# Strassen steps in w_down: where they stand in a group, and how many there are

## The reference, cut to what matters

```python
def conv_ffn(h, w_up, conv_w, conv_b, w_down):
    u = h @ w_up
    ...                                    # depthwise convolution of width 3 over tokens
    gate, val = jnp.split(y, 2, axis=-1)   # 5632 columns each
    return (jax.nn.silu(gate) * val) @ w_down
```

## Time and profile before

| | us |
|---|---|
| median of three runs | 2383.92 |
| lowest and highest | 2383.77, 2384.22 |
| profiled execution, whole | 2383.82 |
| its span in the trace | 2382.0 |

### The profile page before, as it was taken

The page is one execution under the profiler, slowest core; times in us unless marked ns, Lnnn a source line. Parts: engine busy times, 40 slices in busy tenths (PEclk is TensorE's granted clock), DMA queues, the critical chain, the costliest instruction groups (busy, mean ns, idle before and its releaser), DMA issues.

```text
span 2382.0 us, 30675 instructions
## 1 busy us (share of the span) xinstructions
PE 2376.1 (100%) x12581; PEld 2034.5 (85%) x12581; DVE 1700.7 (71%) x1804; ACT 1217.8 (51%) x1427; POOL 0.2 (0%) x4
## 2 busy tenths in 40 slices
PE   9999999999999999999999999999999999999999
PEld 8888888888888888888888888888888888888887
DVE  6565666666568868868768667855778778886788
ACT  5444454554545445445445555555555455545554
POOL 0000000000000000000000000000000000000000
PEclk9999999999999999999999999999999999999999
DMA  7566556565565665655665555555555655565555
GB/s 253 160 187 196 166 186 196 191 188 196 187 186 178 219 215 186 216 182 197 200 192 189 184 185 160 170 184 186 186 182 192 201 189 174 186 219 187 187 173 181
DMA packets 238039, 452.14 MB, mean 190 GB/s; under 512 B 16569, under 2 KB 20779, under 8 KB 237771
## 3 DMA queue, kind: packets, MB, share of 16 engines
q1 hardware_dynamic: 237147, 449.07, 58.1%
q10 hardware_dynamic: 752, 1.12, 0.1%
HBM read 446.46 MB, written 3.67 MB: 189 GB/s over the span
## 4 chain that ended last, share of the span: by engine, by line
PE 97%; DVE 2%; ACT 1%; DMA 0%; issue 0%; SPq 0%; DVEq 0%; ACTq 0%
PE PS L72 97%; DVE WL L72 1%; ACT WH L72 0%; DVE PT L72 0%; DMA RAW<-in_w_in 0%; DVE TB L72 0%; DVE PB L72 0%; DVE TA L72 0%; ACT TB L72 0%; DVE TC L72 0%; DVE SEL L72 0%; DVE MHL L72 0%; ACT TA L72 0%; DVE XT L72 0%; SPq L72 0%
## 5 line engine op out<-in xcount | busy, mean ns | idle before, releaser
L72 DVE TENSOR_TENSOR WL<-RAW,WH 128x1024 fp32r<-128x1024 f32 (+1 forms) x844 | 1002.0, 1204 | 513.5 <-ACT WH L72 511.1
L72 PE MATMUL PS<-XHL,WH 128*128 128x512 f32 x3984 | 1252.7, 396 | 0.3 <-DVE XHL L72 0.3
L72 ACT ACTIVATE WH<-RAW 128x1024 fp32r<-128x1024 f32 (+1 forms) x845 | 868.9, 1043 | 736.6 <-PE PS L72 723.4
L72 PEld LDWEIGHTS PS<-XHL,WL 128*128 128x128 f32 x3968 | 745.4, 188 | 176.0
L72 PE MATMUL PS<-XHL,WL 128*128 128x256 f32 x3968 | 779.7, 278 | 0.0
L72 PE MATMUL PS<-WH,MHL 128*128 128x512 f32 x2000 | 624.0, 390 | 0.0
L72 PEld LDWEIGHTS PS<-XHL,WH 128*128 128x128 f32 x3984 | 606.6, 188 | 4.4 <-issue 0.8
L72 PEld LDWEIGHTS PS<-WH,MHL 128*128 128x128 f32 x2000 | 375.4, 188 | 77.7
L72 PE MATMUL PS<-WL,MHL 128*128 128x512 f32 x1000 | 389.1, 389 | 0.0
L72 PEld LDWEIGHTS PS<-WL,MHL 128*128 128x128 f32 x1000 | 187.8, 188 | 38.3
L72 ACT ACTIVATE MHL<-TA 128x1024 fp32r<-128x1024 f32 x33 | 35.1, 1063 | 121.7 <-DVE TA L72 121.7
(11 more groups left out here) (150 smaller groups left out, 1211.6 us busy)
## 6 DMA issues: line engine op xcount, KB each, us to landing
RAW<-in_w_ff SPq DMA_DIRECT2D x256, 512.0 KB, 4.2
RAW<-in_w_in SPq DMA_DIRECT2D x224, 512.0 KB, 3.8
RAW<-in_w_up SPq DMA_DIRECT2D x176, 512.0 KB, 4.3
RAW<-in_w_down SPq DMA_DIRECT2D x88, 512.0 KB, 4.5
RAW<-in_w_mix_out SPq DMA_DIRECT2D x32, 512.0 KB, 3.9
RAW<-in_w_out SPq DMA_DIRECT2D x32, 512.0 KB, 3.6
RAW<-in_w_conv_out SPq DMA_DIRECT2D x16, 512.0 KB, 3.5
RAW<-in_w_attn_out SPq DMA_DIRECT2D x16, 512.0 KB, 4.3
```

Of the source, the lines that this page charges most:

```text
L72: ins = step[1](*step[2], **step[3])
```

## The change

The table `SEVEN` gets one tuple of pairs for each of the two groups of a part, instead of one for both. In ff both are as before. In the second and third part the steps move from the fifth and sixth pair to the fourth and sixth in the first group, and to the second, fourth and sixth in the other. In the short part the first group keeps its step at the fourth pair, and the second group gets one at the second pair beside it. The sums of activations are made for the union of both groups' pairs (`union`), each in a slot of its own: AXH and AXL have three slots instead of two, and AS moves into SQ to make room.

```diff
-SEVEN = {"ff": (2, 4), "down8": (4, 5), "down6": (3,)}
+SEVEN = {"ff": ((2, 4), (2, 4)), "down8": ((3, 5), (1, 3, 5)), "down6": ((3,), (1, 3))}
...
-            AXH = sb("AXH", [P, 2, 4, P], f32r, c=c)
-            AXL = sb("AXL", [P, 2, 4, P], f32r, c=c)
-            AS = sb("AS", [P, 4, P], c=c)
+            AXH = sb("AXH", [P, 3, 4, P], f32r, c=c)
+            AXL = sb("AXL", [P, 3, 4, P], f32r, c=c)
             EV = sb("EV", [P, 2, 512], c=c)
-            sb("QK2pad", [P, 4096 - 1536 - 2048], c=c)
...
+        AS = SQ[:].rearrange("p (a b) -> p a b", a=4)
...
+        def union(name):
+            return sorted({n for g in SEVEN[name] for n in g})
+
-        def pairs(w, row0, kcs, col0, name):
+        def pairs(w, row0, kcs, col0, name, g):
...
-                    seven = n in SEVEN[name]
+                    seven = union(name).index(n) if n in SEVEN[name][g] else None
                     steps.append((seven, len(ents), kcs[2 * n:2 * n + 2]))
-                    if seven:
+                    if seven is not None:
                         ents.extend((what, first) for what in ("left", "b22", "t13", "t24"))
...
-            sevens = [n for n, st in enumerate(steps) if st[0]]
+            sevens = [n for n, st in enumerate(steps) if st[0] is not None]
...
-                    i = sevens.index(n)
+                    i = seven
                     o, c = n == sevens[0], n == sevens[-1]
...
-            for i, pair in enumerate(SEVEN[name]):
+            for i, pair in enumerate(union(name)):
                 if pair // 2 == half_seg:
                     sums_x(i, 2 * (pair % 2), tok, after)
                     yield
```

More of the change, by code:

```diff
@@ L238, in weight_order @@
                 for g in range(2 if seg < 3 else 1):
-                    pairs(io["w_ff2"][0], 2048 * seg, k16, 1024 * g, "ff")
+                    pairs(io["w_ff2"][0], 2048 * seg, k16, 1024 * g, "ff", g)
             for g in (2, 3):
@@ L258, in weight_order @@
                     pairs(io["w_down_2"][0], 512 * g0, list(range(4 * (g1 - g0))), 1024 * g,
-                          f"down{2 * (g1 - g0)}")
+                          f"down{2 * (g1 - g0)}", g)
             return len(units)
@@ L511, in group_item @@
             mid = dict(mid)
-            sevens = [n for n, st in enumerate(steps) if st[0]]
+            sevens = [n for n, st in enumerate(steps) if st[0] is not None]
             ends = [None, None]
             for n, (seven, e, kcs) in enumerate(steps):
-                if not seven:
+                if seven is None:
                     for half in range(2):
@@ L603, in sums_x @@
             v = V.step(tt, AS[:, 3, :], a12, AS[:, 1, :], sub)
-            a = A.step(act, AXH[:, seven], AS[:], AF.Copy, after=[v, ax_free.get(seven)])
-            tok[seven] = V.step(tt, AXL[:, seven], AS[:], AXH[:, seven].bitcast(f32), sub, after=[a])
+            a = A.step(act, AXH[:, seven], AS, AF.Copy, after=[v, ax_free.get(seven)])
+            tok[seven] = V.step(tt, AXL[:, seven], AS, AXH[:, seven].bitcast(f32), sub, after=[a])
         def group(w, row0, kcs, g, name):
-            steps = pairs(w, row0, kcs, 1024 * g, name)
+            steps = pairs(w, row0, kcs, 1024 * g, name, g)
             group_col[id(steps[0])] = 1024 * g
```

## The result

| | before | after |
|---|---|---|
| median of the unprofiled runs, us | 2384.04 | 2393.64 |
| lowest and highest, us | 2383.77, 2385.09 | 2390.47, 2394.07 |
| profiled execution: whole, span, us | 2383.82, 2382.0 | 2393.97, 2392.2 |

The change costs 9.6 us. The ratio is 1.0037, 95% interval 1.0026 to 1.0048. I had forecast 2388.9, half of that, and a range up to 2391.2. The sign and the place are as forecast; a second cost comes on top of the wait.

A forecast was written before the change was run, and what follows sets the result against it. The prediction took PE to bound the kernel. Matmuls saved (-2.04), stalls won (-1.1) and waits for PSUM (+8.2) gave +5.06 us on 2383.82, so 2388.9 us, range 2385.5 to 2391.2.

The forecast's parts named there:

- the nine matmuls: PE, whole kernel: three more Strassen steps, each three matmuls or 0.68 us less, take off 2.04 us.
- The two stalls: w_down, first groups of second and third parts: PE's waits for WL shrink, winning 0.54 and 0.56 us, together 1.1.
- The wait for PSUM: Second groups' second pair: PE waits for DVE to empty four banks, 2.67, 2.19 and 3.37 us, together 8.2.
- E: Start of DVE's emptying of the first group's last step; 1834.62 us forecast in the short part, later events counted from it.
- The clock: Behind the second groups' waits: no cost in the sum; every us at the lower level would cost half a us.
- rival 4: Second pair: wait grows by a late load, 0.5 to 1.2 us a part, or clock falls; 2390.4 to 2392.4, chance 0.12.
- Rivals 2 and 3: Second pair: no wait, 2380.5 us, chance 0.08 (2); half of the wait, 2385.0 us, chance 0.13 (3).
- The chances of sign: Whole kernel: slower by over 0.2% (above 2388.7 us) 0.52, within 0.2% 0.46, faster 0.02.

The follow-up runs named there:

- third_pair: Changed kernel with the second groups' first step at the third pair instead of the second, as many steps: 2381.81 us, ratio 0.9990 to the kernel before.
- moves_only: Changed kernel without added steps: fourth and sixth pair in both groups of the long parts, short part as before: 2382.88 us, ratio 0.9994 to before.
- after_again: The changed kernel itself, run and traced once more: 2394.07, 2393.76, 2390.62, 2390.57 and 2394.12 us.
- The filler kernels: Changed kernel with 8 or 4 matmuls of zeros in the wait before the second group's first step: 2389.47 us with 8, 2389.11 with 4.
- evac_first: Changed kernel with the first group's banks emptied before the split of t13 enters DVE's queue: 2384.00 us, ratio 1.0000 to the kernel before.
- spread4: third_pair with the long parts' second group at third, fifth and sixth pair, and a fourth slot for activation sums: 2382.90 us, ratio 0.9995 to before.
- short_only: Changed kernel with the long parts' steps as before; only the short part has its additional step: 2386.1 us, ratio 1.0011 to the kernel before.

## Why the prediction was wrong

**The bound, and the nine matmuls.** Right. PE is the bound, and steps without a wait are worth what was summed: the short part of third_pair lasts 1873.50 - 1810.23 = 63.27 us, 0.67 less than in before, where 0.68 was forecast.

**The two stalls.** Right: 1.1 us forecast, 1.2 measured in moves_only. The third part's stall went whole, where 0.2 us of it was expected to stay.

**The wait for PSUM.** Right in place and size. DVE's order came out as it was worked out, from the short part's E = 1836.27: the split at E + 2.85 (2.85 forecast), the new sum at + 4.20 (4.20), the emptying at + 13.02 (12.91), PE's restart at + 15.64 (15.65). In the third part E + 16.11 (16.13). Without the lower clock the three parts cost +2.12 (the short part of after_again), +1.06, and 51.08 + 39.59 - 88.59 = +2.08 us, where 39.59 is the rest of a third part at full clock: 2382.0 - 2341.84 in before, less the 0.68 of the step, plus the 0.11 of the restart. The sum is 5.3 us; forecast were 5.06. The filler kernels say the same as whole times: 2389.1 and 2389.5 us, against 2388.9. Part by part the forecast was 1.99, 0.97 and 2.13, so it is not the luck of a sum.

**The clock.** This is the step that failed: the sum put the clock behind the waits at nothing. It stood in rival 4 alone, with a chance of 0.12 for all of that rival, and how long it would be low was not worked out. The reason given was the granted clock of 1.00 at the start, where PE idled 1.04 of 4 us. That was a misreading: there the table has no record to show, and the matmuls of that stretch lie 0.21 us apart where the same ones later lie 0.11 apart. The only row that seemed to speak for a full clock beside idle time came from a stretch at half speed.

The text also said that no row showed a gap so long. The trace of before has one, at its end. PE's last matmul ends at 2378.72, and the stretch table gives 0.68 for 2380.00 to 2382.00, which puts the fall at 2380.7, 2.0 us later. It costs nothing there, but it would have told that a pause of 2 us can be enough. With it the term should have been priced from both sides, at nothing and at half speed behind each wait. It cost 1.59 us in the short part (67.65 - 66.06) and 1.70 in the third (92.37 - 51.08 - 39.59), 3.3 us in the traced execution. The medians, 2393.6 against 2389.1 to 2389.5 with the gap filled, differ by 4.2 to 4.5 us, which hold the late start too.

The Trainium skill (TensorE: Matmul & The Clock Gate, section Why this matters for your kernels) speaks of gaps longer than about 3 us. No gap here was that long and the clock fell all the same, so the measurement decides: 1.90 us was enough in some of the cases.

**The late start.** Not forecast. It is 1.65 us of the 10.2 between the two traces. It is the lower clock as well, at the start of the program instead of behind a wait, and rows 9 hid it by the same 1.00. The change is not needed for it, since the traces of evac_first and spread4 have it too, and by their times some executions of moves_only and of the kernel before. It is present in every traced execution of the changed kernel, and by the prices in those near its median too, while in the kernel before it came in 5 of 27 by their times. So some 1.6 of the 9.6 us between the medians are its share by this account; why it comes so often beside two falls was not found.

**Rivals.** Rivals 2 and 3 (no wait, or half of it) are refuted by the XT rows. Rival 4's other half, a late load in front of the sum, did not occur: in all three parts PB starts 1.35 us after the split ahead of it (1839.12 and 1840.47 in the short one), as without a load to wait for. The chances of sign (0.52 slower, 0.46 within 0.2%) leaned on 2388.9 being so near to the border of 2388.7; with the clock priced, most of the chance would have been above it.

In short: 5.3 us of waits less savings, 3.3 us of lower clock behind two waits and 1.65 us of lower clock at the start make the 10.2 us between the two traces.

## What to carry to other kernels

Before work is put early in a stage, ask which buffer it borrows and who empties that: here PE needed four banks 5.4 us after the last use, and the engine that empties them had three splits of the same step queued in front. Two lines of order in DVE's queue took back what w_down had lost, 8.5 us of 8.6. A gap in a PE-bound kernel can cost more than its length: price the slower matmuls behind it as well, or fill it. And check a table's clock against the distance of matmuls of one shape before you lean on it.

## What the runs showed of the hardware

- A gap of 1.9 us in a stream of matmuls brought the lower clock in 3 of 7 traced cases, short_only's among them, a gap of 2.4 us in 3 of 3, gaps of 1.01 to 1.49 us in none of 3. Each fall cost about 1.6 us: the matmuls lie 0.42 to 0.43 us apart instead of 0.23 for some 3 us.
- In all six the fall comes after the gap, not in it, 0.1 to 1.3 us behind PE's restart. In the short part of after six matmuls start from 1851.91 to 1853.18, the last five 0.23 us apart, and only then does the distance grow to 0.43.
- Matmuls of zeros in the gap kept the clock up in all three parts, 4 calls being enough (8 matmuls in the trace, 1.05 us together).
- The kernel starts at half speed: 128x128 matmuls lie 0.21 us apart, and 0.11 later. Full speed came by 4.4 to 5.9 us in seven traces and at 9.1 to 10.5 us in five, and in these five the first projection is 1.1 to 1.9 us later than in before. The mean granted clock doesn't show it: it stays at 1.000, because this time has no record.
